# Both routers of a two-block model without the filler matmuls between TensorE's waits

## The chip, the core and the metric

The kernel runs on one core of a Trainium2 chip, as one launch. The metric is the time of one execution on the device in microseconds (us), the lower the better. Everything is computed in float32. A core has a matrix engine (PE, TensorE), a vector engine (DVE, VectorE), an activation engine (ACT, ScalarE), a general engine (POOL, GpSimd) and a queue engine (SP, SyncE) that here does little but start DMAs. Each engine runs its own instructions in order; they meet at semaphores. TensorE's clock has two levels, 2.4 GHz and 1.2 GHz, and the profile shows which of them was granted in any stretch.

## The reference

Two blocks run one after the other on 256 tokens of width 1024 (the first block puts 16 meta tokens ahead of them, 272 in all). The first has two layers, each a mixer and then a mixture of experts; the second has a state-space mixer and a latent-attention mixer, each with an MLP. The part that the change touches is the expert router:

```python
def hierarchical_moe(h, w_group, b_group, w_expert, b_expert, w_gate, w_up, w_down):
    glog = xf @ w_group + b_group                      # 4 groups
    g = jnp.argmax(glog, axis=-1)
    elog = (xf @ w_expert).reshape(T, 4, 8) + b_expert # 8 experts in a group
    elog_g = elog of group g
    vals, loc = lax.top_k(elog_g, 2)
    gates = softmax(glog)[g] * jax.nn.softmax(vals, axis=-1)
    ...
    hb = jax.nn.silu(xb @ w_gate[e]) * (xb @ w_up[e])   # each expert on its own tokens
    ys = hb @ w_down[e]
    ...
for i in range(2):                                     # first block
    mixed = rglru_mixer(h, ...) if i == 0 else shortconv_mixer(h, ...)
    h = layer_norm(ALPHA * h + mixed, ...)
    h = layer_norm(ALPHA * h + hierarchical_moe(h, ...), ...)
```

## The kernel before

The weights stream through `ring`, six slots of 2 MB in on-chip memory, in the order of a plan. An expert's gate, up and down matrix take three slots, so the ring holds two experts; a third (`EXTRA`, expert 5) has room of its own in `work`. SP starts the load of a slot as soon as the instruction that used it last has signalled (L532 in the trace): the gate and up matrices of expert 2 go into the slots of expert 0 and wait for the end of expert 0's `gate_up`.

Each of the two layers `l` of the first block runs through the same steps. The mixer's output projection (`rows_out`, L769) ends with token block 1 and then token block 2. DVE makes the layer norm of each block (L1820 to L1805) as its half is done; the last instruction of a block's norm is L1805, and it sets `mix{l}_normed`. Then comes `moe(l)`, first its router, on PE in this order:

- For each token block: `transposes` (L735) turn the normed rows in two halves, ACT copies each half to `hT` (L1495), and `logits` (L902 and the bias in L904) multiplies them with the 36 routing columns. A logits matmul loads 128 columns of weights and streams 36. Layer 0 has the small meta block too, whose logits come after those of block 1.
- DVE (`route(l)`, L1891 to L1916) chooses group and two experts for each token and sets `choice{l}`.
- PE adds up ranks (L928) and totals (L932); DVE waits for the ranks (L1923), makes the slots of the tokens and the one-hot matrices up to L1835, and sets `slots_of_tokens{l}`.
- PE gathers the rows of the first four experts with the one-hot matrices (`pick_rows`, L820, 512 columns each), turns them (`turn_rows`, L827), and starts expert 0 (`gate_up`, L792).

`keep_busy(n)` (L891) issues n matmuls that nothing reads: weights `before`, 288 moving columns of the routing weights, into PSUM bank 5. It stands in the router at four places, and at two places outside it (n of 1 and 6) that stay. A float32 matmul other than a transpose shows in the trace as two records, so n fillers are 2n records there.

The order of work on each engine is the order of the code; no scheduler moves anything.

Of the kernel before, what the change touches and what calls it, by code (L numbers as in the profile page):

```python
# [73 lines left out]
def first_and_second_block(nc, a, out):  # L74
# [4 lines left out]
    with ctx:  # L79
# [60 lines left out]
        def S(name):  # L140

            name = shared.get(name, name)
            if name not in sems:
                sems[name] = nc.alloc_semaphore(name)
            return sems[name]

        def nth(name, count):

            return S(name), base.get(name, 0) + count
# [572 lines left out]
        def _(pe):  # L722
            def transposes(n, blocks, hold, only=None, bank=0):

                for i, b in enumerate(blocks):
                    if only is not None and i != only:
                        continue
                    m = BLOCKS[b][1]
                    pe.wait_ge(*nth(hold, i + 1)) if hold else pe.wait_ge(*nth(f"x_loaded{b}", 16))
                    for h in range(2):  # L730
                        j = 2 * i + h
                        if j >= 2:
                            pe.wait_ge(*nth(f"{n}_hT", j - 1))
                        for c in range(4):
                            mm = pe.transpose(ps[:, bank + j % 2, c * P:c * P + m], hres[0:m, b, (4 * h + c) * P:(4 * h + c + 1) * P],  # L735
                                              ident[0:m, 0:m])
                        mm.then_inc(S(f"{n}_turned"), 1)
# [150 lines left out]
            def keep_busy(n):  # L888

                for _ in range(n):  # L890
                    pe.matmul(ps[:, 5, 0:288], before[:, :], w_route[:, 1, :, :].rearrange("p k n -> p (k n)"), start=True, stop=True)  # L891

            def moe(l):
# [3 lines left out]
                def logits(i):  # L897
                    b = blocks[i]
                    t0, m = BLOCKS[b]
                    out_ = ps[0:m, 7, 36 * i:36 * i + 36]  # L900
                    for k in range(DC):
                        pe.matmul(out_, hT[:, k, t0:t0 + m], w_route[:, l, k, :], start=(k == 0 and b == 1), stop=False,  # L902
                                  skip_group_check=True)
                    return pe.matmul(out_, ones[0:1, 0:m], b_route[0:1, l, :], start=False, stop=(i == nb - 1),  # L904
                                     skip_group_check=True)
# [4 lines left out]
                for i in range(nb):  # L910
                    transposes(f"mix{l}", blocks, f"mix{l}_normed", only=i)
                    if blocks[i] >= 1:
                        if blocks[i] == 1:
                            keep_busy(2)
                            pe.wait_ge(*nth(f"mix{l}_var", nb))
                        pe.wait_ge(*nth(f"mix{l}_hT", 2 * i + 2))
                        mm = logits(i)
                    if blocks[i] == 1:
                        if l == 0:
                            logits(0)  # L920
                        keep_busy(2 if l == 0 else 3)
                mm.then_inc(S(f"logits{l}"), 1)

                keep_busy(8)
                pe.wait_ge(*nth(f"choice{l}", 1))
                o = rowb[:, 800:800 + 32 * nb]
                for d_ in range(nb):
# [5 lines left out]
                                   skip_group_check=True)  # L933
                mm.then_inc(S(f"totals{l}"), 1)

                keep_busy(5)
                pe.wait_ge(*nth(f"slots_of_tokens{l}", 1))
                for h in range(2):
                    pick_rows(l, blocks, h, 6 - h)
# [181 lines left out]
            pe.wait_ge(*nth("lru_evac", 16))  # L1121
            rows_out("mix0", [1, 2], ["lru_out0", "lru_out1"], lru_y, 0, "lru_z", meta_rows_out)
            moe(0)

            t_first = NMETA - NTAIL
# [35 lines left out]
            pe.wait_ge(*nth("sc_z", DC - 1))  # L1161
            rows_out("mix1", [1, 2], ["sc_out0", "sc_out1"], sc_z, NMETA, "sc_z")
            moe(1)

            b_map = ring[:, place["s5_tab1"], :].rearrange("p (s i n) -> p s i n", s=ST, i=2)
# [1477 lines left out]
```

## Time and profile before

| | |
|---|---|
| time, 3 runs | 1858.6, 1861.74, 1863.37 us, median 1861.74 |
| profiled execution | time 1863.29 us, span from first to last instruction 1861.6 us |
| busy share of the span | PE 84%, weight loads (PEld) 54%, DVE 41%, ACT 12%, POOL 4% |
| mean granted TensorE clock | 0.919 of full speed |
| DMA | 540.12 MB, mean 290 GB/s |
| filler matmuls (L891) | 84 records in the whole span |

The span is cut by the expert stages: about 155 to 610 us is that of layer 0, about 765 to 1210 us that of layer 1. The routers lie just ahead of each, about 122 to 151 us and 732 to 761 us. Times below are microseconds from the start of the span, and a granted clock of 1.00 is 2.4 GHz, 0.50 is 1.2 GHz. PE's busy time counts a matmul from start to modelled end and says little on its own here; the routers are read from what waits for what.

### The profile page before, as it was taken

To read this page: it belongs to the slowest core of one execution; us is meant where nothing else is said; L and a number is where in the kernel's file an instruction comes from. 1 tells how busy PE (TensorE), PEld (TensorE's weight loads), DVE (VectorE), ACT (ScalarE), POOL (GpSimd) and SP (SyncE) were. 2 spreads that over 40 slices of the span, in tenths; PEclk is the share of its full clock that TensorE was granted. 3 is DMA by queue.
4 is the path that set the end of the run, shared out by engine and by line. 5 is a ranking of instruction groups with operands and counts; after the bars stand their busy time and mean duration, and the time that the engine had idled before them with its cause. 6 is when DMAs were issued, how large, how long until landed. Compare 5 with 4: busy or idle time off the path is not lost. (4 is left out here: it accounts for less than half of the span.)

```text
span 1861.6 us, 29604 instructions
## 1 busy us (share of the span) xinstructions
PE 1564.0 (84%) x13201; PEld 1013.8 (54%) x13201; DVE 756.7 (41%) x1571; ACT 218.2 (12%) x496; POOL 75.9 (4%) x95
## 2 busy tenths in 40 slices
PE   8999868788876899885656575689999999999998
PEld 6654434444443785542323232378699545769843
DVE  5853123443124313313311110180476653566756
ACT  2311011011110100100110000011000002400000
POOL 2000000000000100000000000051000001000000
PEclk9998988888998899888887887899999999999999
DMA  9366999999998938599999999955444434325420
GB/s 331 125 265 258 426 378 424 424 425 425 424 426 354 381 136 361 229 422 423 421 419 407 427 418 422 388 206 218 153 172 163 161 126 162 136 91 183 180 90 23
DMA packets 88077, 540.12 MB, mean 290 GB/s; under 512 B 7343, under 2 KB 9455, under 8 KB 54157
## 3 DMA queue, kind: packets, MB, share of 16 engines
q1 hardware_dynamic: 86060, 531.24, 70.9%
q0 software_dynamic: 1888, 6.95, 1.0%
q8 instruction: 107, 1.75, 0.4%
q14 instruction: 22, 0.17, 0.0%
HBM read 531.89 MB, written 6.29 MB: 289 GB/s over the span
## 5 line engine op out<-in xcount | busy, mean ns | idle before, releaser
L792 PE MATMUL ps<-ring,work 128*32 128x256 f32 x3968 | 300.3, 465 | 216.5 <-DMA ring<-in_moe_w_up 215.7
L792 PEld LDWEIGHTS ps<-ring,work 128*32 128x32 f32 x3968 | 156.2, 129 | 347.8 <-issue 294.2
L2170 DVE TENSOR_TENSOR rowb<-rowb,ps 128x128 f32<-128x128 f32 x64 | 18.4, 287 | 380.1 <-ACT rowb L1590 380.1
L2176 DVE COPY multi<-ps 128x256 f32<-128x256 f32 x64 | 27.2, 425 | 265.9 <-PE ps L805 265.8
L805 PE MATMUL ps<-ring,multi 128*32 128x256 f32 x1984 | 123.1, 390 | 12.6 <-ACT multi L1595 11.4
L743 PE MATMUL ps<-hT,ring 128*128 128x258 f32 (+2 forms) x528 | 118.9, 386 | 0.0
L1307 PE MATMUL ps<-ring,work 128*128 128x512 f32 x256 | 114.4, 592 | 0.0
L769 PE MATMUL ps<-ring,work 128*128 128x512 f32 x256 | 110.9, 593 | 0.0
L743 PEld LDWEIGHTS ps<-hT,ring 128*128 128x128 f32 x528 | 99.7, 190 | 18.9 <-issue 2.9
L805 PEld LDWEIGHTS ps<-ring,multi 128*32 128x32 f32 x1984 | 59.1, 111 | 75.0 <-issue 25.0
L1272 PE MATMUL ps<-hT,ring 128*128 128x128 f32 x768 | 95.4, 275 | 1.5 <-ACT hT L1495 1.5
L1272 PEld LDWEIGHTS ps<-hT,ring 128*128 128x128 f32 x768 | 90.4, 192 | 2.0 <-ACT hT L1495 2.0
L1307 PE MATMUL ps<-work 128*128 128x512 f32 x192 | 87.0, 592 | 0.0
L1590 ACT ACTIVATE rowb<-ps 128x128 f32<-128x128 f32 x64 | 17.8, 278 | 551.8 <-PE ps L792 551.8
L820 PE MATMUL ps<-hres,rowb 128*128 128x512 f32 (+1 forms) x160 | 81.3, 631 | 0.2 <-DVE rowb L1835 0.2
L769 PEld LDWEIGHTS ps<-ring,work 128*128 128x128 f32 x256 | 48.4, 190 | 60.6 <-issue 60.3
L1307 PEld LDWEIGHTS ps<-ring,work 128*128 128x128 f32 x256 | 48.5, 190 | 60.3 <-issue 60.3
L835 PE MATMUL ps<-multi,tmp_a 32*128 32x256 f32 x1024 | 73.3, 400 | 1.1 <-DVE multi L2176 1.1
L835 PEld LDWEIGHTS ps<-multi,tmp_a 32*128 32x128 f32 x1024 | 46.2, 184 | 30.4 <-issue 26.9
L1272 PE MATMUL ps<-rowb,work 128*128 128x128 f32 x512 | 62.5, 275 | 0.0
L1307 PEld LDWEIGHTS ps<-work 128*128 128x128 f32 x192 | 36.5, 190 | 45.9 <-issue 45.9
L1272 PEld LDWEIGHTS ps<-rowb,work 128*128 128x128 f32 x512 | 59.7, 192 | 0.2 <-DVE tmp_a L2494 0.2
(503 smaller groups left out, 1921.2 us busy)
## 6 DMA issues: line engine op xcount, KB each, us to landing
ring<-in_moe_w_gate SPq DMA_DIRECT2D x62, 2048.0 KB, 18.2
ring<-in_moe_w_up SPq DMA_DIRECT2D x62, 2048.0 KB, 23.1
ring<-in_moe_w_down SPq DMA_DIRECT2D x62, 2048.0 KB, 22.4
ring<-in_w_ff SPq DMA_DIRECT2D x32, 2048.0 KB, 8.0
ring<-in_sc_w_in SPq DMA_DIRECT2D x6, 2048.0 KB, 17.7
ring<-in_ssm_w_glu SPq DMA_DIRECT2D x4, 2048.0 KB, 19.1
ring<-in_lru_w_in SPq DMA_DIRECT2D x3, 2048.0 KB, 14.5
ring<-in_lru_w_out SPq DMA_DIRECT2D x2, 2048.0 KB, 23.5
```

What stands on the lines that cost most here:

```text
L743: mm = pe.matmul(ps[:, bank, 0:n], w[:, k, P * c:P * c + P], hT[:, k, t0:t0 + n], start=(k == 0), stop=(k == DC - 1))
L769: mm = pe.matmul(ps[0:m, 2 + 2 * b + hf, :], left[:, kk, t0:t0 + m], w[:, k, 512 * hf:512 * hf + 512], start=(kk == 0), stop=(kk == 4 * la ...
L792: mm = pe.matmul(ps[32 * q:32 * q + 32, bank, 0:256].rearrange("p (u n) -> p u n", u=2), x[:, k, :], gu[:, k, :, 2 * P * (q // 2):2 * P * ...
L805: mm = pe.matmul(ps[32 * q:32 * q + 32, bank, 0:256], hT_[:, 32 * k:32 * k + 32], w[:, k, 256 * q:256 * q + 256], start=(k == 0), stop=(k ...
L820: mm = pe.matmul(ps[:, bank, :], one_hot[0:m, i, 0:P], hres[0:m, b, 4 * P * h:4 * P * h + 4 * P], start=(i == 0), stop=(i == len(blocks) - 1))
L835: mm = pe.matmul(ps[:, q, SEQ * (b - 1):SEQ * b], w[r, t0:t0 + P], y[r, :], start=(first and b == 1), stop=False, skip_group_check=True)
L1272: mm = pe.matmul(pair_part(j, i), w[:, k, :], x[:, k, :], start=(k == 0), stop=(k == 3), skip_group_check=True)
L1307: mm = pe.matmul(ps[:, product_bank[i], :], left[:, k, :], right[:, k, :], start=(j == 0 and k == 0), stop=(j == 7 and k == 1))
L1590: A(silu[b], ps[:, 4 + b, 0:P], ACT.Silu).then_inc(S(f"silu{l}"), 1)
L2170: V.tensor_tensor(hid[b], silu[b], ps[:, 4 + b, P:2 * P], ALU.mult).then_inc(S(f"hid_ready{l}"), 1)
L2176: V.tensor_copy(y_out[b], ps[:, 4 + b, 0:256]).then_inc(S(f"y_ready{l}"), 1)
```

## The change

All four `keep_busy` calls in the router go, for both layers. The two that stand outside the router stay, and nothing else differs.

```diff
@@ moe(l), router
                     if blocks[i] >= 1:
                         if blocks[i] == 1:
-                            keep_busy(2)
                             pe.wait_ge(*nth(f"mix{l}_var", nb))
                         pe.wait_ge(*nth(f"mix{l}_hT", 2 * i + 2))
                         mm = logits(i)
                     if blocks[i] == 1:
                         if l == 0:
                             logits(0)
-                        keep_busy(2 if l == 0 else 3)
                 mm.then_inc(S(f"logits{l}"), 1)
 
-                keep_busy(8)
                 pe.wait_ge(*nth(f"choice{l}", 1))
...
                 mm.then_inc(S(f"totals{l}"), 1)
 
-                keep_busy(5)
                 pe.wait_ge(*nth(f"slots_of_tokens{l}", 1))
```

On PE, layer 0's router from the end of the meta block's logits to the gathering of rows, before (names are output<-inputs, then partitions x columns and the count of matmuls):

```order
L904 MATMUL ps<-b_route,ones 16x36
L891 MATMUL ps<-w_route,before 128x288 x2
L735 MATMUL ps<-ident,hres 128x128 x8
L902 MATMUL ps<-w_route,hT 128x36 x8
L904 MATMUL ps<-b_route,ones 128x36
L891 MATMUL ps<-w_route,before 128x288 x8
L928 MATMUL ps<-rowb,before 128x96
L928 MATMUL ps<-rowb,ones 128x64
L928 MATMUL ps<-rowb,ones 128x32
L932 MATMUL ps<-rowb,ones 128x32 x3
L891 MATMUL ps<-w_route,before 128x288 x5
L820 MATMUL ps<-hres,rowb 128x512 x6
```

And the same place on PE after the change (the lines below the edit have moved up by up to four numbers):

```order
L904 MATMUL ps<-b_route,ones 16x36
L735 MATMUL ps<-ident,hres 128x128 x8
L902 MATMUL ps<-w_route,hT 128x36 x8
L904 MATMUL ps<-b_route,ones 128x36
L925 MATMUL ps<-rowb,before 128x96
L925 MATMUL ps<-rowb,ones 128x64
L925 MATMUL ps<-rowb,ones 128x32
L929 MATMUL ps<-rowb,ones 128x32 x3
L820 MATMUL ps<-hres,rowb 128x512 x6
```

The fillers stood between pieces of router work and no other instruction has changed its place. In layer 0 they are 2, 2, 8 and 5 matmuls, in layer 1 they are 2, 3, 8 and 5, so 35 matmuls or 70 records of 84 go. Layer 1's router on PE, before:

```order
L904 MATMUL ps<-b_route,ones 128x36
L891 MATMUL ps<-w_route,before 128x288 x3
L735 MATMUL ps<-ident,hres 128x128 x8
L902 MATMUL ps<-w_route,hT 128x36 x8
L904 MATMUL ps<-b_route,ones 128x36
L891 MATMUL ps<-w_route,before 128x288 x8
L928 MATMUL ps<-rowb,before 128x64
L928 MATMUL ps<-rowb,ones 128x32
```

After the change the two stretches of fillers between these rows are empty, and the transposes (L735) and the ranks (L925 now) come straight behind the waits that the code puts ahead of them:

```order
L904 MATMUL ps<-b_route,ones 128x36
L735 MATMUL ps<-ident,hres 128x128 x8
L902 MATMUL ps<-w_route,hT 128x36 x8
L904 MATMUL ps<-b_route,ones 128x36
L925 MATMUL ps<-rowb,before 128x64
L925 MATMUL ps<-rowb,ones 128x32
```

## Rows read from the trace of the kernel before

**Rows 1.** Windows: stretch, length, busy us (records) of five engines, PEclk, DMA share, GB/s

```profile
136.00:155.00 19.00, 18.32 (x119) 10.25 (x118) 8.18 (x40) 3.77 (x6) 0.00 (x0) 0.97 0.00 1
156.00:600.00 444.00, 349.73 (x3986) 192.10 (x3989) 145.33 (x396) 50.39 (x117) 8.51 (x12) 0.87 1.00 415
...
766.50:1190.00 423.50, 271.42 (x3458) 144.37 (x3460) 86.07 (x208) 41.38 (x91) 3.62 (x5) 0.83 1.00 420
```

**Rows 2.** Timeline, router of layer 0 and behind: start, us, engine, instruction, idle before

```profile
125.55 1.98 PE L902 MATMUL ps<-w_route,hT 128*128 128x36 f32 x16
...
127.05 2.07 DVE L1805 SCALAR_TENSOR_TENSOR hres<-tmp_a,mean_var,multi 128x1024 f32<-128x1024 f32 x1
...
128.57 1.24 PE L891 MATMUL ps<-w_route,before 128*128 128x288 f32 x4
...
129.65 1.04 PE L735 MATMUL ps<-ident,hres 128*128 128x128 f32 x8
...
131.42 1.98 PE L902 MATMUL ps<-w_route,hT 128*128 128x36 f32 x16 [0.74 <-ACT hT L1495]
...
134.21 0.17 DVE L1891 TENSOR_REDUCE tmp_a<-ps 128x3 f32<-128x12 f32 x1 [4.48 <-PE ps L904]
...
139.34 0.26 DVE L1916 TENSOR_TENSOR rowb<-rowb 128x96 f32<-128x96 f32 x1
...
140.61 0.35 DVE L1923 TENSOR_TENSOR rowb<-rowb,ps 128x192 f32<-128x192 f32 x1 [0.86 <-PE ps L928]
...
143.91 6.00 PE L820 MATMUL ps<-hres,rowb 16*128 16x512 f32 x12 [0.23 <-DVE rowb L1835]
...
155.08 0.34 SPq L532 DMA_DIRECT2D ring<-in_moe_w_gate  x1
...
170.08 0.33 SPq L532 DMA_DIRECT2D ring<-in_moe_w_gate  x1
```

**Rows 3.** Timeline of the router of layer 1

```profile
737.12 2.08 DVE L1805 SCALAR_TENSOR_TENSOR hres<-multi,mean_var 128x1024 f32<-128x1024 f32 x1
...
740.94 1.16 PE L735 MATMUL ps<-ident,hres 128*128 128x128 f32 x8
...
745.39 7.11 PE L891 MATMUL ps<-w_route,before 128*128 128x288 f32 x16
745.57 0.17 DVE L1891 TENSOR_REDUCE tmp_a<-ps 128x2 f32<-128x8 f32 x1 [5.74 <-PE ps L904]
...
749.92 0.23 DVE L1916 TENSOR_TENSOR rowb<-rowb 128x64 f32<-128x64 f32 x1
...
752.98 0.29 DVE L1923 TENSOR_TENSOR rowb<-rowb,ps 128x128 f32<-128x128 f32 x1 [2.68 <-PE ps L928]
...
755.66 3.69 PE L820 MATMUL ps<-hres,rowb 128*128 128x512 f32 x8
```

**Rows 4.** Windows around three falls of the granted clock, columns as in rows 1

```profile
130.20:133.60 3.40, 2.66 (x23) 2.38 (x21) 0.00 (x0) 2.37 (x3) 0.00 (x0) 1.00 1.01 426
133.60:137.00 3.40, 3.40 (x9) 2.50 (x9) 2.43 (x13) 0.21 (x1) 0.00 (x0) 0.50 0.26 108
745.50:751.40 5.90, 5.90 (x13) 4.18 (x14) 4.11 (x22) 0.41 (x2) 0.00 (x0) 0.50 0.00 0
```

**Rows 5.** Timeline of PE behind the experts of layer 0

```profile
613.84 1.97 PE L735 MATMUL ps<-ident,hres 128*128 128x128 f32 x8 [1.01 <-DVE hres L2255]
```

**Rows 6.** Weight loads of two lines: duration in ns, min/median/max

```profile
L1134 PEld LDWEIGHTS ps<-rowb,ones x2: 333/335/337, 615.4 to 615.6; 128*128 128x128 f32 x2
...
L932 PEld LDWEIGHTS ps<-rowb,ones x10: 192/192/192, 140.3 to 753.0; 128*128 128x128 f32 x10
```

**Rows 7.** Windows: the stretch of rows 5, and two restarts after a wait

```profile
612.20:616.00 3.80, 2.75 (x12) 2.60 (x12) 2.70 (x8) 0.75 (x2) 0.00 (x0) 0.50 1.06 389
164.80:167.70 2.90, 2.90 (x29) 1.33 (x32) 2.13 (x9) 0.28 (x1) 0.00 (x0) 0.50 1.02 429
267.90:273.50 5.60, 5.60 (x56) 2.96 (x60) 0.00 (x0) 0.00 (x0) 0.00 (x0) 0.50 1.04 434
```

## The prediction

> **What bounds the kernel now.** I read three views. The windows come first, to see what the DMA engines do about the routers. From 136 to 155 us they move nothing, and then they are busy at a share of 1.00 from 156 to 600 us and again from 766.5 to 1190 us [rows 1]. So the expert stages end when the weights have come in, and each of these streams starts with one instruction: SP's load at 155.08 us, which waits for the end of expert 0's `gate_up` [rows 2]. The ring is full until then. A router that ends x us later starts the stream x us later, and since PE waits for the stream and everything behind waits for PE, x is paid in full; a router that ends earlier gives it back in full. What TensorE does in the router's waits matters only through the time at which this one load starts.
>
> The timeline comes second: who holds the router up. In layer 0 the second block's norm is ready at 127.05 + 2.07 = 129.12 us, PE transposes at 129.65, ACT copies, PE makes the logits from 131.42, DVE starts at 134.21 and has the choice at 139.34 + 0.26 = 139.60, PE adds ranks, DVE goes on at 140.61, and the gathering of rows starts at 143.91 [rows 2]. It is a chain PE, ACT, PE, DVE, PE, DVE, PE in which each waits for the one before. The fillers lie in PE's waits, and where a wait is over before the fillers are, they hold the chain up. In layer 0 that is a little at one place: the filler batch of 128.57 ends at 129.81, after the norm. In layer 1 it is much at two: the norm is ready at 737.12 + 2.08 = 739.20 but the transposes start at 740.94, and the choice is ready at 749.92 + 0.23 = 750.15 but 16 filler records last from 745.39 to 752.50, so that DVE goes on only at 752.98 [rows 3].
>
> The third view is the granted clock. From 130.2 to 133.6 us, in which PE did transposes, a wait and logits and no fillers, it stood at 1.00, and from 133.6 to 137.0 at 0.50, which is 1.2 GHz; in layer 1 it was 0.50 from 745.5 to 751.4, and that is why those fillers took 7.11 us [rows 3, 4]. So a stretch of router work without fillers has been followed by the lower level already, and the fillers that came next brought the clock back before the gathering of rows.
>
> **The change part by part.** 35 matmuls go, 70 records. None is waited for. Two things follow: the delays that they cause end, and the clock stays low for longer. No DMA, semaphore or instruction of another engine is touched, so DVE's and ACT's own parts stay as they are.
>
> What the lower level costs for each kind of work: eight transposes took 1.97 us at 0.50 and 1.04 at 1.00, so +0.9 [rows 2, 5, 7]. Logits and ranks stream few columns and are bound by their weight loads. A load of 128 columns took 335 ns at the low level and 192 ns at the high one, a factor of 1.7 [rows 6, 7]; the matmuls themselves can at most double. Gathering streams 512 columns, so I double it.
>
> The Trainium skill ("TensorE: Matmul & The Clock Gate", section "LDWEIGHTS (loading the stationary operand)") gives a weight load a time of its columns over 1.2 GHz, with no term for the level, an estimate of 107 ns for 128 columns either way. By it the logits and ranks would not slow at all. The trace disagrees: the load is 1.7 times longer at the low level [rows 6], and I go by the trace.
>
> *Layer 0.* (a) Start of the second block's transposes. The logits ahead of them take 125.55 to 128.57 us, 3.0 us [rows 2]. If the clock holds, PE is ready before the norm and starts about 129.3: -0.35. If it falls as they begin, they last 3.0 x 1.7 = 5.1 us, to 130.7: +1.05. Nothing says where the fall comes; I take the middle, +0.35. (b) Transposes at the low level: +0.9. (c) Logits and bias, 131.42 to about 133.7, 2.3 us by a factor of 1.7: +1.6, at most double, +2.3. (d) Ranks: DVE went on 1.01 us after the choice, of which 0.7 are weight loads and matmuls: +0.5, at most +0.9. The totals behind them delay nobody, since PE waits again anyway. (e) Gathering. After a long wait the clock is low when PE starts again. How long it then worked at the low level: 2.9 us at 164.8 and 5.6 us at 267.9 [rows 7]. Half of that is lost, 1.5 to 2.8 us, middle 2.2. The 6.00 us of gathering [rows 2] are long enough to hold all of it, so `gate_up` would run at the high level as before. Sum of the middles: 0.35 + 0.9 + 1.6 + 0.5 + 2.2 = +5.6; of the low ends +4.1 (with -0.35, 0.9, 1.6, 0.5, 1.5), of the high ends +8.0.
>
> *Layer 1.* (a) The fillers of 3 go: the start moves from 740.94 to between 739.4 and, with slow logits ahead, 739.7: -1.4. (b) Transposes took 1.16 us, now 1.97: +0.8. (c) as above: +1.6, at most +2.3. (d) Choice to DVE took 752.98 - 750.15 = 2.83 us; in layer 0, where no filler was in the way, 1.01. The delay of 1.8 goes and the low level adds 0.5: -1.3, at worst -0.9. (e) +2.2; the gathering is 3.69 us long [rows 3], so it can hold 2.8 too. Sum of the middles: -1.4 + 0.8 + 1.6 - 1.3 + 2.2 = +1.9; low end about +0.8, high end about +4.2.
>
> Together +7.5 us, between +4.9 and +12.2. The sum stands against the profiled execution, 1863.29 us; its span is 1861.6. The median of the three runs is 1.55 us lower than that execution, so the forecast is 1861.74 + 7.5 = 1869.2, rounded to 1869 us, +0.4%.
>
> **Rivals.** *The clock costs nothing that counts.* If logits and ranks went on at their old pace and the gathering found the clock high, only the delays would be left: -0.35 in layer 0, -1.5 and -1.8 in layer 1, together -3.7, 1858.1 us. It is decided by the clock at the logits and at the start of the gathering. For it: the low level is followed by no visible loss where PE only waits. Against it: rows 4 show the fall behind just such work, and the change leaves nothing in the waits of 5 and 3 us. Even so it would be faster by 0.2%, less than about 0.3% (5.6 us), which a measurement of this kernel can tell from no change. A chance of 0.14, a third of it beyond 0.3%.
>
> *Weight loads don't slow, the gathering does.* The page's rule as a mechanism here: terms (c) and (d) lose 1.6 + 0.5 in each layer, 4.2 us, which leaves +3.3, 1865.0 us, no change that can be told. Against it are rows 6, though only two records stand on one side of them. A chance of 0.12.
>
> *A gap in the stream.* The load of expert 3's gate starts at 170.08 us, at the end of expert 1's `gate_up` [rows 2]. The stream from 155.08 brings 6 MB ahead of it, at the 415 GB/s of rows 1 15.2 us, so until 170.3. The margin is 0.2 us: if expert 0's and 1's stretch, of which 2.9 us were at 0.50 [rows 7], is low for a further 3 us, about 1.5 us are added in layer 0, and if it is low throughout, some 4: 1871 to 1873 us. A chance of 0.12. If it were high throughout, nothing is won, since the DMA engines are full.
>
> *The clock stays low through the gathering and expert 0.* From the end of gathering at 149.91 to the load at 155.08 are 5.2 us, of which I count 4 as `gate_up`. Then the 6.00 and 3.69 us and these 4 us in each layer double: +17.7 in place of 4.4, 1882.5 us. Speaking against it is that every restart of rows 7 came back within 5.6 us of work. A chance of 0.05.
>
> **How the numbers follow.** The forecast has the remaining 0.57, with its own range of 1866.6 to 1873.9; since 0.3% lies at 1867.3, a tenth of this is within it. Slower by over 0.3%: 0.51 + 0.12 + 0.05, and some 0.02 of the weight load's case; 0.70. Within: 0.06 + 0.10 + 0.09; 0.25. Faster: 0.05. The range runs from 1860.5, which leaves out most of the first rival, to 1877, which takes in the high end and most of the gap; the two ends leave out 0.1 each.
>
> **What would show it.** In the changed kernel's windows: clock 0.50 from the second block's logits to the start of gathering in both routers, and 3 to 6 us more. In its timeline: about 3.7 us instead of 2.3 for logits and bias of block 2, 1.5 instead of 1.0 from choice to DVE in layer 0, 8.2 instead of 6.0 us of gathering; and in layer 1 the transposes within 0.5 us of the norm. From the second norm of layer 0 (129.12) to the load at 155.08 are 25.96 us, which should become 31.5. DMA share in both expert stages stays 1.00. The prediction is wrong if the clock is high when the gathering starts, if logits don't stretch, or if something else than expert 0's `gate_up` starts the stream.

## The result: 0.35% slower, and the profile after

| | before | changed |
|---|---|---|
| time, 11 runs each | 1856.36 to 1864.28, median 1859.01 us | 1864.34 to 1870.96, median 1866.60 us |
| profiled execution, time and span | 1863.29, 1861.6 us | 1866.88, 1865.1 us |
| mean granted clock | 0.919 | 0.914 |

The ratio is 1.0035 with a 95% interval of 1.0025 to 1.0046, which is 6.5 us (4.6 to 8.6); the two medians are 7.6 us apart. Of the runs behind the ratios of the experiments below, one of the kernel with 24 late fillers (2150 us) and one of the kernel before (8551 us) were far slower than all the others and are left out.

The timeline of layer 0's router in the changed kernel (columns as in rows 2; L1801 is the norm, L1887 and L1912 enclose the choice, L1919 takes the ranks):

```profile
123.01 2.06 DVE L1801 SCALAR_TENSOR_TENSOR hres<-tmp_a,mean_var,multi 128x1024 f32<-128x1024 f32 x1
...
124.38 0.27 PE L904 MATMUL ps<-b_route,ones 1*16 1x36 f32 x2
...
125.13 1.97 PE L735 MATMUL ps<-ident,hres 128*128 128x128 f32 x8 [0.47 <-DVE hres L1801]
...
127.78 3.63 PE L902 MATMUL ps<-w_route,hT 128*128 128x36 f32 x16 [0.69 <-ACT hT L1491]
...
132.45 0.17 DVE L1887 TENSOR_REDUCE tmp_a<-ps 128x3 f32<-128x12 f32 x1 [6.75 <-PE ps L904]
...
137.58 0.26 DVE L1912 TENSOR_TENSOR rowb<-rowb 128x96 f32<-128x96 f32 x1
...
139.48 0.35 DVE L1919 TENSOR_TENSOR rowb<-rowb,ps 128x192 f32<-128x192 f32 x1 [1.50 <-PE ps L925]
...
142.79 8.70 PE L820 MATMUL ps<-hres,rowb 16*128 16x512 f32 x12 [2.13 <-DVE rowb L1831]
...
156.64 0.34 SPq L532 DMA_DIRECT2D ring<-in_moe_w_gate  x1
...
170.08 0.33 SPq L532 DMA_DIRECT2D ring<-in_moe_w_gate  x1
```

The same instructions as in [rows 2] are longer: transposes 1.97 us in place of 1.04, logits 3.63 in place of 1.98, gathering 8.70 in place of 6.00. DVE's own stretch from L1887 to the end of L1912 is 5.39 us in both. In layer 1, where the norm was ready at 740.39:

```profile
740.44 1.97 PE L735 MATMUL ps<-ident,hres 128*128 128x128 f32 x8 [1.13 <-DVE hres L1801]
...
743.10 3.63 PE L902 MATMUL ps<-w_route,hT 128*128 128x36 f32 x16 [0.69 <-ACT hT L1491]
...
753.20 0.29 DVE L1919 TENSOR_TENSOR rowb<-rowb,ps 128x128 f32<-128x128 f32 x1 [1.07 <-PE ps L925]
...
755.86 5.40 PE L820 MATMUL ps<-hres,rowb 128*128 128x512 f32 x8 [1.92 <-DVE rowb L1831]
```

The windows of the changed kernel (columns as in rows 1): the first four cover layer 0's router and its expert stage, the last three layer 1's.

```profile
121.00:124.40 3.40, 2.89 (x35) 2.74 (x36) 3.26 (x5) 0.44 (x2) 0.00 (x0) 1.00 0.95 405
124.50:148.30 23.80, 14.60 (x46) 9.86 (x44) 10.93 (x55) 2.89 (x5) 0.00 (x0) 0.50 0.26 107
148.40:156.60 8.20, 7.95 (x80) 3.93 (x79) 0.00 (x0) 3.56 (x5) 0.00 (x0) 1.00 0.01 2
157.50:600.00 442.50, 345.18 (x3989) 191.74 (x3992) 145.28 (x396) 50.39 (x117) 8.50 (x12) 0.89 1.00 417
...
738.90:759.20 20.30, 11.82 (x40) 9.11 (x41) 10.41 (x51) 2.89 (x5) 0.00 (x0) 0.50 0.32 136
759.40:766.40 7.00, 6.75 (x78) 3.46 (x77) 0.00 (x0) 3.56 (x5) 0.00 (x0) 1.00 0.01 2
768.50:1190.00 421.50, 270.89 (x3441) 143.81 (x3440) 85.13 (x208) 41.38 (x91) 3.63 (x5) 0.83 1.00 418
```

TensorE is at 1.2 GHz without a break for 23.8 us and 20.3 us, from before block 2's transposes until 5.5 and 3.3 us into the gathering. In the kernel before, the same places had one low stretch of 3.4 us in layer 0 and two in layer 1, of 3.4 and 6.8 us (rows 4 show the first and most of the last). Expert 0 starts at the high level and the DMA engines are full in both expert stages, as before [rows 1].

Taking the router from the second norm to SP's load apart, in us:

| | layer 0 before | after | layer 1 before | after |
|---|---|---|---|---|
| norm to transposes | 0.53 | 0.06 | 1.74 | 0.05 |
| transposes to DVE's start (transposes, ACT, logits) | 4.56 | 7.32 | 4.63 | 6.96 |
| choice to DVE's next (ranks) | 1.01 | 1.64 | 2.83 | 1.22 |
| start of gathering to `gate_up` | 7.28 | 9.96 | 4.96 | 6.68 |
| norm to load | 25.96 | 31.57 | 25.31 | 26.04 |

The rest (choice, slots, `gate_up`) is the same within 0.02 us. The two routers are 5.6 and 0.7 us longer, 6.3 together, well inside the measured interval. The spans of the two profiled executions are only 3.5 us apart, mainly because the one of before was 4.05 us later at its first router (129.12 against 125.07 us at the norm), which has nothing to do with the change. Part of it is a fall of the clock:

```profile
27.90:34.50 6.60, 6.23 (x18) 3.57 (x20) 4.17 (x9) 2.75 (x5) 1.52 (x4) 0.50 1.04 268
```

That window is of the kernel before, and this one of the changed kernel, over the same code:

```profile
25.50:28.80 3.30, 2.98 (x10) 1.59 (x11) 3.09 (x7) 0.81 (x1) 1.47 (x3) 0.50 1.08 270
```

Two executions of the same code had a low stretch of 6.6 and of 3.3 us near the start. From just ahead of these stretches to just behind them the lag grew from 2.45 to 4.04 us, so the clock accounts for 1.6 us of it. The first 2.45 us arose before 20 us, where the first 32 matmul records of L1074 (L1070 in the changed kernel) took 9.82 and 7.60 us, with a recorded clock of 1.00 in both; the cause of that is open. Single executions therefore differ by some us in unchanged code, and below the routers are compared in the traces and the times over many runs.

One more stretch of unchanged code differs, behind the routers: the first two experts of layer 0. In the kernel before:

```profile
157.60:167.80 10.20, 8.50 (x75) 3.86 (x77) 6.29 (x17) 1.35 (x2) 0.00 (x0) 0.50 0.98 419
171.10:174.10 3.00, 2.63 (x42) 1.71 (x45) 0.00 (x0) 0.28 (x1) 0.00 (x0) 1.00 0.85 330
```

and in the changed kernel:

```profile
171.10:174.10 3.00, 2.63 (x41) 1.70 (x45) 0.00 (x0) 0.28 (x1) 0.00 (x0) 1.00 1.03 437
```

In the kernel before the clock was low for 10.2 us there, the load of expert 3's gate started 15.0 us after the first one instead of 13.4, and the DMA engines ran at 330 GB/s for 3 us, in place of 437. By these rates the stream of before lost about 0.7 us (an estimate), which the changed kernel did not lose.

### The profile page after: what moved, and what is told of

The parts are those of the page before. It is cut to its first block and busy times, and to the rows that moved or that the text cites. A ratio compares the mean times of both kernels' runs of the same rounds, so it can differ in the third digit from the quotient of the medians.

```text
span 1865.1 us, 29464 instructions
## 1 busy us (share of the span) xinstructions
PE 1545.8 (83%) x13131; PEld 1003.2 (54%) x13131; DVE 754.2 (40%) x1571; ACT 218.3 (12%) x496; POOL 75.7 (4%) x95
## 5 line engine op out<-in xcount | busy, mean ns | idle before, releaser
L2172 DVE COPY multi<-ps 128x256 f32<-128x256 f32 x64 | 27.2, 425 | 264.4 <-PE ps L805 264.4
```

Source lines behind the costliest of these rows:

```text
L2172: V.tensor_copy(y_out[b], ps[:, 4 + b, 0:256]).then_inc(S(f"y_ready{l}"), 1)
```

## The experiments

Each is the kernel before with the edit shown; `keep_busy(0)` stands where fillers are gone. Ratios are to the kernel before on the same chip.

**One layer alone: where is the loss?** First layer 0's fillers away.

```diff
-keep_busy(2)
+keep_busy(2 if l == 1 else 0)
-keep_busy(2 if l == 0 else 3)
+keep_busy(0 if l == 0 else 3)
-keep_busy(8)
+keep_busy(8 if l == 1 else 0)
-keep_busy(5)
+keep_busy(5 if l == 1 else 0)
```

> Only layer 0's 17 fillers are gone, layer 1's stay. Clock theory: layer 0's router from the second norm to SP's first load of the stream lasts 31.6 us instead of 26.0 (as in the changed kernel), layer 1's stays at about 25.3, and the time is 5.6 us longer, ratio 1.0030. Rival (the loss is spread evenly, or lies elsewhere than in the router): about 3 us, or a router interval that doesn't move.

Measured: 1.0037 (1.0024 to 1.0051), 6.9 us. Layer 0's router took 32.71 us, 1.1 us more than in the changed kernel with the same code, because here the clock fell during the logits of block 1 (2.94 us) and the transposes started 1.15 us after the norm. Layer 1's, whose code is unchanged, took 23.66 us, not 25.3.

The mirror image, only layer 1's fillers away:

> Only layer 1's 18 fillers are gone. Clock theory: the delays that the fillers caused (1.7 us at the transposes, 1.6 at the ranks) and the slower work nearly cancel, layer 1's router lasts 26.0 us instead of 25.3, time +0.7 us, ratio 1.0004, not to be told from 1. Rival (the low clock costs the same in both routers): +3 us or more, ratio 1.0017.

Measured: 1.0014 (1.0002 to 1.0025), 2.6 us; layer 1's router took 26.29 us. Layer 0 carries most of the loss, as the theory said, but the time doesn't exclude the rival's 3 us for layer 1. The traces show how much one execution can differ: layer 1's router with its fillers took 25.31 us in one and 23.66 in the other, without them 26.04 and 26.29. The 25.31 is no unusual value, though. The stretch from the norm to the moment at which DVE has its ranks contains both delays of the fillers, and five kernels have layer 1's fillers unchanged up to there. It is 13.8 us in three of them (before, with 8 late fillers, without the last 5), 14.87 with 24 late fillers and 12.11 here; without the fillers it is 12.81 us in both traces. In layer 0 it is 11.5 us in five of six kernels with the fillers and 13.12 in one, and without them 14.41 and 15.50. An estimate of the mean price from these traces is 6 us in layer 0 and 1 us in layer 1; the times of this kernel allow 0.4 to 4.7 us for layer 1.

**The instructions or what they stream?** All fillers stay, but each streams 2 columns.

```diff
+def small(n):
+    for _ in range(n):
+        pe.matmul(ps[:, 5, 0:2], before[:, :], w_route[:, 1, 0, 0:2], start=True, stop=True)
...
-keep_busy(8)
+small(8)
```

(and so at the other three places)

> All 35 fillers stay as instructions with their 128-column weight load, but stream 2 columns instead of 288. Clock theory: what counts is the streaming, so the clock falls as in the changed kernel, both routers last about 31.5 and 26 us, time +6 us, ratio 1.0035. Rival (any instruction keeps PE awake, its count or its weight load is enough): clock and time as before, or up to 4 us faster because these fillers are short and hold nothing up.

Measured: 1.0050 (1.0030 to 1.0070); routers 31.71 and 26.14 us, those of the changed kernel to 0.14 us. Its window over the stretch in which the changed kernel was low:

```profile
124.50:148.30 23.80, 20.67 (x76) 16.33 (x74) 10.90 (x55) 2.89 (x5) 0.00 (x0) 0.50 0.25 106
```

and a piece of its timeline in it:

```profile
132.19 3.57 PE L891 MATMUL ps<-w_route,before 128*128 128x2 f32 x16
138.17 0.74 PE L933 MATMUL ps<-rowb,before 128*128 128x96 f32 x2 [2.40 <-DVE rowb L1921]
```

PE has 20.67 us of busy time here where the changed kernel had 14.60, and the clock is 0.50 all the same. In layer 1 it was 0.50 from 738.9 to 759.2 us, too. So neither the instructions in the queue nor PE's busy time as the profile counts it is what the fillers bring; the rival is out.

**Is a late start of the stream paid in full?** Fillers behind the wait for the slots, where everything waits for PE.

```diff
 keep_busy(5)
 pe.wait_ge(*nth(f"slots_of_tokens{l}", 1))
+keep_busy(8)
```

> All fillers stay and 8 more follow behind the wait for the slots, ahead of the gathering, where PE is the one that is waited for. 16 records at 0.27 us: each router is 4.3 us longer. Theory that a later start of the stream is paid in full: +8.6 us, ratio 1.0046. Rival (slack in the expert stages or behind them takes it up): under half of it, ratio below 1.0023.

Measured: 1.0025 (1.0013 to 1.0038), 4.7 us (2.4 to 7.1), a miss against the 8.6 that were expected. The routers were 4.1 and 3.9 us longer in the trace, as the added fillers should make them, so some 3 us of 8 did not arrive. The same with 24:

> As the run with 8 late fillers, which cost 4.1 and 3.9 us in its two routers but only 4.7 us in time, now with 24 late fillers in each router: 48 records at 0.267 us are 12.8 us a router, 25.6 us together. Theory that a later stream is paid in full and the missing 3 us there were scatter of the stages behind: +24 to +27 us, ratio 1.0130 to 1.0145. Rival (there is slack that takes up about 3 us): +22 to +23 us. Rival (a fixed share of 40% is absorbed): +15 us, ratio 1.008.

Measured: 1.0126 (1.0105 to 1.0146), 23.4 us (19.5 to 27.2); routers 37.80 and 38.05 us, 24.6 longer together. A fixed share of 40% is out. Between the two kernels lie 17.1 us of fillers (64 records at 0.267), and their ratios differ by 18.7 us. So the delay goes through at about full price between 8 and 24; the interval of the 24 holds both theories for the 3 us that are missing with 8. The traces say a little more. From the first load of layer 0's stream to layer 1's second norm it took 584.12 us before, 582.88 with 8 late fillers and 581.95 with 24, so 1.2 and 2.2 us of layer 0's delay of 4.1 and 11.8 were made good on the way. In the traces of the other kernels it lies between 582.8 and 584.6 us, so the 1.2 may be scatter and the 2.2 lie just outside of it. The 0.7 us of the stream that the kernel before lost can be part of it: with 8 late fillers the DMA engines moved 437 GB/s from 170.5 to 173.5 us, behind the load of expert 3's gate, where the kernel before had 330. What is shown is that most of a router's delay is paid, not that all of it is.

**Which fillers?** Three kernels, each without one group in both routers.

```diff
-keep_busy(2)
+keep_busy(0)
-keep_busy(2 if l == 0 else 3)
+keep_busy(0)
```

> Only the fillers around the logits of block 1 are gone (2 and 2 in layer 0, 2 and 3 in layer 1); the 8 and the 5 stay. Clock theory: the clock falls before the transposes and logits of block 2, which last 0.9 and 1.6 us longer in layer 0; the 8 fillers then start at 1.2 GHz, last 6 to 7 us where the wait is 5.4 (layer 0) and 4.6 us (layer 1), and hold the ranks up by 1 to 2 us; but they bring the clock back, and the gathering is as fast as before. Layer 0 +3.5 us, layer 1 (which saves 1.7 us at the transposes) +0.5 us: +4 us, ratio 1.0022. Rival (what counts is only the clock at the gathering): 0 to +0.5 us.

Measured: 1.0001 (0.9990 to 1.0013). A miss: nothing where 4 us were expected. Its PE in layer 1's router:

```profile
737.56 1.97 PE L735 MATMUL ps<-ident,hres 128*128 128x128 f32 x8 [1.30 <-DVE hres L1805]
740.22 3.63 PE L902 MATMUL ps<-w_route,hT 128*128 128x36 f32 x16 [0.69 <-ACT hT L1495]
743.78 0.64 PE L904 MATMUL ps<-b_route,ones 1*128 1x36 f32 x2
744.35 5.53 PE L891 MATMUL ps<-w_route,before 128*128 128x288 f32 x16
749.71 0.33 PE L928 MATMUL ps<-rowb,before 128*128 128x64 f32 x2
...
753.03 3.69 PE L820 MATMUL ps<-hres,rowb 128*128 128x512 f32 x8
```

The transposes start 0.05 us after the norm, and the logits are slow (3.63 us), both as foreseen. But the 8 fillers took 5.53 us here, not 7.11 [rows 3], and the ranks came 1.6 us sooner after the choice than in the trace before; the router was 24.38 us, less than before. In layer 0 (27.83 us) the logits of block 2 ran at the high level, since the clock had come back by then. Together the two routers of this execution were 1.0 us longer than before's. The early fillers buy fast logits and pay for them with the delays that they cause.

```diff
-keep_busy(8)
+keep_busy(0)
```

> Only the 8 fillers ahead of the choice are gone, in both routers. Clock theory: the clock falls at the second logits as it did before, nothing brings it back until the 5 fillers behind the ranks, which take 5 us at 1.2 GHz where the wait is 3.3 (layer 0) and 2.7 us (layer 1). Ranks +0.6 and the gathering 1.8 and 2.3 us late, part of the restart is paid by the fillers; layer 1 saves the 1.6 us that the 8 held up. Together +3 to +5 us, ratio 1.002. Rival (the 8 fillers are what keeps the gathering fast): the gathering itself is slow as in the changed kernel, +8 us.

Measured: 1.0028 (1.0017 to 1.0039), 5.2 us. In layer 0, where the router took 31.16 us:

```profile
137.54 0.74 PE L928 MATMUL ps<-rowb,before 128*128 128x96 f32 x2 [5.92 <-DVE rowb L1916]
...
140.12 5.15 PE L891 MATMUL ps<-w_route,before 128*128 128x288 f32 x10
145.20 6.22 PE L820 MATMUL ps<-hres,rowb 16*128 16x512 f32 x12
```

The 5 fillers behind the ranks took 5.15 us where the wait is 3.3, and the gathering, at 6.22, was fast: the delay lies ahead of it, as expected, and the rival is out. Of the 5.2 us by which this router is longer, 1.6 arose ahead of the missing fillers, from a fall of the clock at the transposes (1.91 us, and 1.28 us after the norm). Layer 1's router took 25.21 us, no longer than before's, since the delay of its ranks is gone.

```diff
-keep_busy(5)
+keep_busy(0)
```

> Only the 5 fillers between the ranks and the gathering are gone, in both routers. Clock theory: the 8 fillers have brought the clock to 2.4 GHz; the wait of about 3 us without work may or may not let it fall at the start of the gathering, so each gathering lasts as before or is up to 1.7 us longer: 0 to +3.4 us, middle +1.8, ratio 1.0010. Rival (these 5 are the ones that count for the gathering): both gatherings as slow as in the changed kernel, +2.7 and +1.7 us, ratio 1.0024.

Measured: 1.0007 (0.9998 to 1.0016), 1.3 us. The profiled execution was a dear one, with both gatherings slow (8.85 us in layer 0, and 6.69 in layer 1):

```profile
131.50:139.50 8.00, 4.34 (x24) 3.30 (x22) 6.35 (x30) 0.20 (x1) 0.00 (x0) 1.00 0.00 2
139.60:146.30 6.70, 5.89 (x7) 1.85 (x8) 2.60 (x16) 0.07 (x1) 0.00 (x0) 0.50 0.00 0
```

The clock fell during the wait behind the ranks. This is the picture that the rival drew. But the execution took 1864.12 us against a median of 1861.81 over 12 runs, and the rival's ratio of 1.0024 lies outside the interval, so in most executions the price is less than in this one. The three groups add up to 0.0036, the whole change to 0.0035, and the fillers ahead of the choice have the largest part. Each of the three has an interval of about 0.001 either way, so that the sum comes out this well is partly luck.

**Better than both.** The empty wait between transposes and logits gets a filler, and the batches that held the chain up shrink.

```diff
+if blocks[i] == 2:
+    keep_busy(1)
 pe.wait_ge(*nth(f"mix{l}_hT", 2 * i + 2))
...
-keep_busy(2 if l == 0 else 3)
+keep_busy(1 if l == 0 else 2)
-keep_busy(8)
+keep_busy(8 if l == 0 else 6)
```

> Fillers rearranged: one more in PE's wait between the transposes and the logits of block 2, which was empty in both layers; one fewer behind the logits of block 1; 6 in place of 8 ahead of the choice in layer 1. Clock theory: layer 1's transposes and ranks start up to 1.7 and 1.6 us earlier, layer 0's transposes 0.3 us; time -2 to -3.5 us, ratio 0.9985. Rival (with fewer fillers the clock falls elsewhere and takes it back): ratio 1.000 or above.

Measured: 0.9986 (0.9975 to 0.9997), 2.6 us faster than before. Layer 1's router took 22.49 us:

```profile
737.60 1.89 PE L735 MATMUL ps<-ident,hres 128*128 128x128 f32 x8
739.30 0.67 PE L891 MATMUL ps<-w_route,before 128*128 128x288 f32 x2
740.17 1.98 PE L902 MATMUL ps<-w_route,hT 128*128 128x36 f32 x16 [0.20 <-ACT hT L1497]
742.08 0.41 PE L904 MATMUL ps<-b_route,ones 1*128 1x36 f32 x2
742.41 4.87 PE L891 MATMUL ps<-w_route,before 128*128 128x288 f32 x12
747.23 0.43 PE L930 MATMUL ps<-rowb,before 128*128 128x64 f32 x2
```

The norm was ready at 737.02 and the choice at 747.17: the transposes wait 0.58 us for fillers, the ranks 0.06. Layer 0's router took 28.21 us, more than before's 25.96: the 5 fillers behind the ranks met the low clock (4.36 us in place of 2.67, and the gathering 1.4 us later), and the transposes did too (0.8 us). With layer 1's part alone (`l == 1 and blocks[i] == 2`, `keep_busy(2)`, and 8 in layer 0, 6 in layer 1):

> The rearranged fillers in layer 1 alone, layer 0's as before. Theory that the gain of the rearranged kernel is layer 1's, whose router took 22.5 us in place of 25.3 there: -2.8 us, ratio 0.9985. Rival (its gain was a draw of where the clock fell): ratio 1.000.

Measured: 0.9984 (0.9973 to 0.9995), 3.0 us faster, router of layer 1 22.47 us. The rival, a lucky draw with a ratio of 1.000, lies just outside the interval, and the gain is layer 1's; between this version and the one before it the ratios do not decide. Which part of the rearrangement brings how much was not measured apart. With more fillers in both layers (10 and 7 ahead of the choice, 6 and 5 behind the ranks):

> The rearranged fillers in both layers, with more of them where PE still idled: 10 and 7 ahead of the choice, 6 and 5 behind the ranks. Clock theory: fewer falls between the logits and the gathering, ratio 0.9975 to 0.9985, at or below the rearranged kernel. Rival (where the clock has fallen all the same, more fillers hold the chain up for longer): 0.9990 to 1.0005.

Measured: 0.9992 (0.9979 to 1.0006), nothing that can be told from before; the profiled execution had routers of 25.73 and 22.75 us. The ratio lies where the rival expected it, but its interval overlaps with those of the two others, so it decides between neither theory.

## Why the prediction was right

The forecast was +7.5 us, measured were 6.5 (4.6 to 8.6). The forecast of the time itself, 1869 us, is 2.4 us above the median of 1866.6, and 2.7 us of that were in its starting point: the kernel before had its median at 1859.01 over 11 runs, not at the 1861.74 of the first three. By its own steps, in us, the prediction's middle against the difference of the two traces:

| term | layer 0: forecast, measured | layer 1: forecast, measured |
|---|---|---|
| (a) start of the transposes | +0.35, -0.47 | -1.4, -1.69 |
| (b) and (c) transposes and logits | +2.5, +2.76 | +2.4, +2.33 |
| (d) ranks | +0.5, +0.63 | -1.3, -1.61 |
| (e) gathering | +2.2, +2.68 | +2.2, +1.72 |
| sum | +5.6, +5.6 | +1.9, +0.7 |

The mechanism is the one that was foreseen, slow work at 1.2 GHz against the delays of the fillers. That layer 0's sum agrees to the tenth is luck: the start of the transposes was 0.8 us better than forecast, and the other three terms together 0.9 us worse.

- What bounds the kernel: the DMA share stays 1.00 in both expert stages, and the two kernels with late fillers show that a delay of the router comes through. "Paid in full" was too strong: with 8 late fillers 3 us were missing, and with 24 the way to layer 1's norm took 2.2 us less.
- (a): the clock fell only at the end of the meta block's logits (124.4 us), so the slow logits ahead of the transposes that I had allowed for did not occur in this execution. In two other traces they did: with layer 0's fillers away, the same code as here, the logits of block 1 lasted 2.94 us and the transposes started 1.15 us after the norm (+0.6), and with only the early fillers away it was 3.33 us and 1.5 us (+1.0). Both lie inside the forecast of -0.35 to +1.05.
- (b) to (d): the factor of 1.7 for work bound by weight loads was a little low, 3.63 / 1.98 = 1.83 for the logits. The formula for weight loads in the Trainium skill ("TensorE: Matmul & The Clock Gate", section "LDWEIGHTS (loading the stationary operand)"), by which the logits would not have slowed at all, is contradicted by these traces too: the loads of the logits have a median of 192 ns in the kernel before and of 333 ns in the changed kernel's slow logits.
- (e): PE gathered 5.5 us in layer 0 and 3.3 us in layer 1 at the low level, inside the 2.9 to 5.6 us that the restarts of [rows 7] had shown. Half of each is 2.8 and 1.7, which is what was lost.
- Layer 1's sum was 1.2 us too high as measured against the one trace, from all four terms. The same router took 23.66 us in another execution, but most traces with these fillers look like the one of before, so a mean loss of about 1 us is what they suggest; it was not measured closely.
- The range of the sum was added up wrongly. The low terms given for layer 1 make about +1.1 and not +0.8, the high ones +3.8 and not +4.2, which gives +5.2 to +11.8 in place of +4.9 to +12.2. The measured difference lies inside either, in its lower half; the measured median lies at the lower end of the sum's own range of 1866.6 to 1873.9 us, because of the starting point.
- The gap in the stream did not come about; a small one was there before. The prediction counts 2.9 us at the low level in the stretch of experts 0 and 1 [rows 7], but that window is only the end of one of 10.2 us. With it the load of expert 3's gate started 15.0 us after the first one and the DMA engines fell to 330 GB/s for 3 us; in the changed kernel it starts after 13.4 us, and they do not.

The rival that the clock costs nothing (1858.1 us) is out by the interval, the one that only the gathering slows by the logits' 3.63 us, and the one that the clock stays low through expert 0 by the windows, where it is 1.00 from 148.4 and 759.4 us on.

## What to carry to other kernels

Work that nobody reads can be worth its place: where TensorE waits in a chain that releases a saturated stream, work out what the chain costs at both clock levels before taking the filler away. Size each batch so that it still ends inside its wait when it runs at 1.2 GHz, since at that level the same filler becomes the thing that is waited for; here moving one filler into an empty wait and shrinking two batches gained 2.6 to 3.0 us, and taking all away cost 6.5. Compare the times of many runs, and stages of a trace, rather than two spans: the unchanged first 35 us differed by 4 us between two executions. Read a stage from several traces, too: one execution shows one pattern of clock falls, and the same router differed by up to 1.6 us between them.

## What the runs showed of the hardware

- Sixteen 36-column logits records took 1.98 us at 2.4 GHz and 3.63 us at 1.2 GHz, eight transposes 1.04 and 1.97 us. The 128-column loads of the logits went from 192 ns to 333. This work, which is bound by its weight loads, paid a factor of 1.8.
- Fillers of 2 columns left the clock at 0.50 for the whole 23.8 us in which PE counted as busy for 20.67 us; high busy time in the profile did not go with a high clock.
- The same router code took 25.96, 27.58 and 25.98 us in layer 0 and 25.31 and 23.66 us in layer 1 in different executions, with falls of the clock at different places. Whether this is also the source of the 8 us between the fastest and slowest run of the kernel before was not measured.
